# Eight of 206 weight blocks in a fused two-block kernel are loaded by two transfers, of 120 and of 8 partitions

## What is computed

```
def peer_ffn(hn, w_peer_q, sub_keys1, sub_keys2, expert_u, expert_v):
    # each token scores 128 x 128 product keys in 8 heads and keeps the best 16 of each head
    ...
    eidx = ...   # 128 experts of 16384 for each token
    def block(args):
        xt, e, g = args
        act = gelu(einsum('nkd,nd->nk', expert_u[e], xt))
        return einsum('nk,nkd->nd', g * act, expert_v[e])
```

## Time and profile before

| | |
|---|---|
| runs, us | 1340.96 median, 1339.92 to 1342.41 |
| the profiled execution's own time, us | 1340.73 |
| its span in the profile, us | 1339.0 |
| gathers (q0) | 268.45 MB, 48.4% of 16 DMA engines' span |
| weights and other loads (q1) | 112.05 MB, 25.4% |
| busy share of PE, DVE, ACT, POOL | 89%, 66%, 51%, 20% |

### The profile page before, as it was taken

How to read it: one execution, slowest core, us unless ns; L and a number is a source line. 1 busy time by engine, 2 the same in 40 slices (tenths; PEclk the granted TensorE clock), 3 DMA queues, 4 the chain that set the end, 5 groups by cost and what they waited for, 6 DMA issues and landing times.

```text
span 1339.0 us, 19013 instructions
## 1 busy us (share of the span) xinstructions
PE 1189.7 (89%) x6314; PEld 834.0 (62%) x6314; DVE 887.7 (66%) x1938; ACT 683.1 (51%) x1482; POOL 270.3 (20%) x305
## 2 busy tenths in 40 slices
PE   8999988887777878788879878999989999999998
PEld 6898864432222223233334323799989999999986
DVE  6764596667666667776667755576867657666664
ACT  6665555445444445554455543534446675444454
POOL 4000033333333333333333432000000030000000
PEclk9999989999999999899999999999999999999999
DMA  6322479999999999999999999536565346555563
GB/s 243 130 95 81 134 273 421 421 420 420 422 421 421 422 421 416 384 413 422 419 422 420 422 422 388 183 122 185 167 208 185 127 143 203 164 182 178 183 209 105
DMA packets 68652, 382.25 MB, mean 285 GB/s; under 512 B 7761, under 2 KB 7889, under 8 KB 35681
## 3 DMA queue, kind: packets, MB, share of 16 engines
q0 software_dynamic: 36864, 268.45, 48.4%
q1 hardware_dynamic: 31424, 112.05, 25.4%
q10 hardware_dynamic: 288, 0.82, 0.2%
HBM read 380.24 MB, written 1.05 MB: 285 GB/s over the span
## 4 chain that ended last, share of the span: by engine, by line
PE 51%; DMA 30%; DVE 8%; ACT 6%; issue 4%; POOL 0%; another core or an unknown queue 0%; SPq 0%; ACTq 0%; DVEq 0%
DMA work<-in_rows,work 30%; PE ps L572 27%; PE ps L915 9%; PE ps L1012 4%; DVE w_lo L367 2%; DVE work L2118 1%; ACT work L1427 1%; PE ps L606 1%; PE ps L826 1%; ACT work L1420 1%; PE ps L612 1%; PE ps L613 1%; ACT work L1423 1%; ACT w_hi L359 1%; DVE work L2311 1%
## 5 line engine op out<-in xcount | busy, mean ns | idle before, releaser
L915 PE MATMUL ps<-work 128*128 128x512 f32 x1024 | 501.8, 624 | 127.1 <-ACT work L1427 126.6
L2118 DVE CUSTOM_DVE_ANT_0 work<-work,ps 128x1024 f32<-128x1024 f32 x256 | 312.4, 1220 | 213.3 <-DMA work<-in_rows,work 210.2
L915 PEld LDWEIGHTS ps<-work 128*128 128x128 f32 x1024 | 182.6, 194 | 432.8 <-ACT work L1427 279.8
L510 POOL DMA_INDIRECT work<-in_rows,work x256 | 244.2, 954 | 566.4 <-PE ps L915 393.2
L367 DVE TENSOR_TENSOR w_lo<-ring,w_hi 128x1024 fp32r<-128x1024 f32 x206 | 252.4, 1231 | 118.6 <-ACT w_hi L359 117.0
L572 PE MATMUL ps<-x_lo,w_hi 128*128 128x256 f32 (+2 forms) x1224 | 294.0, 283 | 1.8 <-DVE x_lo L384 1.7
L359 ACT ACTIVATE w_hi<-ring 128x1024 fp32r<-128x1024 f32 x206 | 214.4, 1051 | 55.1 <-PE ps L1012 24.5
L1420 ACT ACTIVATE work<-work,peer_root 128x1 f32<-128x1 f32 x256 | 75.1, 294 | 317.9 <-DVE work L2118 316.3
L572 PEld LDWEIGHTS ps<-x_lo,w_hi 128*128 128x128 f32 x1224 | 229.0, 190 | 3.5 <-DVE x_lo L384 2.4
L572 PE MATMUL ps<-x_hi,w_hi 128*128 128x256 f32 (+2 forms) x760 | 187.3, 290 | 3.2 <-DVE w_lo L367 1.5
L572 PEld LDWEIGHTS ps<-x_hi,w_hi 128*128 128x128 f32 x760 | 140.7, 189 | 8.7 <-DVE w_lo L367 3.4
(11 more groups left out here) (364 smaller groups left out, 1238.2 us busy)
## 6 DMA issues: line engine op xcount, KB each, us to landing
ring<-in_stream SPq DMA_DIRECT2D x206, 512.0 KB, 3.7
work<-in_rows,work POOLq DMA_INDIRECT x256
res<-in_tokens SPq DMA_DIRECT2D x4, 272.0 KB, 3.2
gain_rows<-in_gain_rows SPq DMA_DIRECT2D x1, 1024.0 KB, 9.5
out_dram<-work SPq DMA_DIRECT2D x4, 256.0 KB, 2.3
keys_sb<-in_keys SPq DMA_DIRECT2D x1, 512.0 KB, 8.3
work<-in_gain ACTq DMA_DIRECT2D x1, 512.0 KB, 4.1
work<-in_kiwi ACTq DMA_DIRECT2D x1, 288.0 KB, 3.7
```

What stands on the lines that cost most here:

```text
L510: g.indirect_dma_start(out=gathered[:, n % ROWS, :], out_offset=None, in_=rows_dram, in_offset=bass.IndirectOffsetOnAxis(ap=expert[:, n:n ...
L915: last = mm(ps[:, Y_BANK[t] + j, :], diag[:, n % DIAGS, :], gathered[:, n % ROWS, D + 512 * j:D + 512 * j + 512], start=False, stop=k == S ...
L2118: v.tensor_tensor_reduce(R["product"][:, D * (n % 2):D * (n % 2) + D], gathered[:, n % ROWS, 0:D], ps[:, bank:bank + 2, :].rearrange("p b ...
```

## The change

Blocks 40 to 47 are taken out of SyncE's loop and each is loaded by two transfers, one of partitions 0 to 119 and one of partitions 120 to 127, the second on semaphores of its own (`rest_landed`). `split_hi` waits for both.

```
+MOST = P - 8
+SIDE = FIRST["w_in_2_values_0"]
...
+        rest_landed = [sem(f"rest_landed{i}") for i in range(RING)]
...
         def split_hi(act, b, turn=None):
             ...
             act.wait_ge(landed[k], t * 16 + 16 * (b // RING + 1))
+            if turn is None and SIDE <= b < SIDE + 2 * RING:
+                act.wait_ge(rest_landed[k], 16 * ((b - SIDE) // RING + 1))
...
-            for first, end in ((1, late), (late + 2, BLOCKS // RING)):
+            for first, end in ((1, SIDE // RING), (late + 2, BLOCKS // RING)):
                 ...
                 if first == 1:
+                    for b in range(SIDE, late * RING):
+                        sp.wait_ge(w_lo_ready, b + 1 - RING)
+                        sp.dma_start(ring[0:MOST, b % RING, :], stream[b][0:MOST, :]).then_inc(landed[b % RING], 16)
+                        sp.dma_start(ring[MOST:P, b % RING, :], stream[b][MOST:P, :]).then_inc(rest_landed[b % RING], 16)
                     for b in range(late * RING, (late + 2) * RING):
```

## The result

The changed kernel is slower: 1358.98 us, the median of 4 runs (1357.8 to 1361.91), against 1340.86 (1339.92 to 1342.41), the median of the three runs named above and a fourth; the ratio is 1.0136, with an interval of 1.0123 to 1.0149. The prediction was 1336.8 us, in a range of 1334.8 to 1342.8. The sign was wrong, and the time was missed by 22 us. All figures are of executions in the chip's usual state; a single one in a slower state (e12_from_last, 1381.08 us, with a granted TensorE clock of 0.846 in place of the 0.98 to 0.99 of its others) is left out.

The account below looks back on a forecast made before the run. The prediction took the gathers to be bound by the DMA engines, one late engine setting their end. Relieving it gave 3.4 + 2.0 - 1.3 = 4.1 us less, so 1336.8 us, in a range of 1334.8 to 1342.8.

Parts of the forecast that it names:

- What bounds the kernel: During the gathers: DMA engines bind, and one late engine sets the end, finishing about 3.4 us after the next.
- 10.5 worked out: Load of blocks 40 to 47: eight blocks at 1.31 us put 10.5 us on each engine, the late one too.
- No later step is shorter: Dot products after 243 us: an instruction packet lengthens a step by 0.94 us, which is never won back.
- I take the first: Split loads: the spared engine is the late one and sheds eight partitions a block, 10.5 us less work.
- 3.4 + 2.0 us of the sum: Gains in the gathers: 3.4 us until the next engine's end, 2.0 us from the stall at 562 us.
- the stall at 562 us: Gathers, when a gather waits for its buffer and other engines run dry: relief returns 0 to 2.6 us, taken as 2.0.
- The rival that the late engine is another: Split loads: the spared engine is not the late one; 1341.0 us, or 1342.3 with one partition more; chance 0.27.
- the term of a packet's price: Split loads: each partition costs its engine about 0.16 us; one more a block costs the next engine 1.3 us.
- Bytes: none added or removed: Loads of blocks 40 to 47: the split moves the same bytes as before.
- The slower rival: Split loads: small or both transfers fall on few engines, up to 10.4 us more, 1351.4 us; chance 0.06.
- The rule that I weighed as a rival: Split loads: both transfers spread over all 16 engines, so the late one sheds at most 0.6 us: 1340.3 us; chance 0.05.
- What was costed at nothing: SyncE's eight added issues (0.33 us each) and ScalarE's added semaphore (at most 0.3 us) hidden; work after the last row unchanged.

Follow-up runs that it names:

- e12_from_last: Changed kernel, but each of blocks 40 to 47 loaded whole after three small transfers reading rows 120 to 127 into partitions 0, 4 ... 28: 1343.96 us.
- e9_none: Changed kernel, but blocks 40 to 47 not loaded (a 16 x 16 float transfer in place of each): 1331.0 us.
- e14_own3: Changed kernel, but each of blocks 40 to 47 loaded whole after three small transfers of partitions 0, 4, 8: 1339.85 us, one run.
- e17_own5: Changed kernel, but each of blocks 40 to 47 loaded whole after three small transfers of partitions 0, 4 ... 16: 1346.68 us, one run.
- e5_evenodd: Changed kernel, but blocks 40 to 47 split into 64 even and 64 odd partitions: 1341.4 us.
- e18_every4: Changed kernel, but blocks 40 to 47 each loaded by four transfers of 32 partitions, every fourth one: 1341.1 us.
- e3_64_64: Changed kernel, but blocks 40 to 47 split into two halves of 64 neighbouring partitions: 1357.45 us.
- e19_near32: Changed kernel, but blocks 40 to 47 each loaded by four transfers of 32 neighbouring partitions: 1357.85 us.
- e15_own1: Changed kernel, but each of blocks 40 to 47 loaded whole after three small transfers of partition 0 alone: 1341.7 us, one run.
- e6: Changed kernel, but each of blocks 40 to 47 loaded whole after three small transfers of partitions 120 to 127: 1356.6 us.
- e11: Changed kernel, but each of blocks 40 to 47 loaded whole after three small transfers reading rows 0, 4 ... 28 into partitions 120 to 127: 1357.1 us.
- e7: Changed kernel, but each of blocks 40 to 47 loaded whole after three small transfers of partitions 0, 4 ... 28: 1345.47 us.
- e4: Changed kernel, but blocks 40 to 47 each loaded by two transfers of all 128 partitions, half the columns each: 1342.91 us.
- e8: Changed kernel, but each of blocks 40 to 47 loaded whole after three small transfers of partitions 0, 4 ... 24: 1344.89 us.
- e16: Changed kernel, but blocks 40 to 47 each loaded as 64 even, 60 odd and 4 odd partitions: 1349.47 us.

## Why the prediction was wrong

**What bounds the kernel** was read rightly in the main. The gathers are bound by the DMA engines, by one of them alone at the end, and what the blocks carry lies on that path: without them 10.1 us go, of 10.5 worked out (e9_none). Two readings on the way were off, without weight for the sum's sign: "No later step is shorter" is not so (12 of the steps after 243 us are under 2.44 us, the shortest 1.56; each follows one that was longer than 2.48 by about as much or more, so the 0.94 us do stay), and the late engine stands some 4 us behind the next and not 3.4, since by rows 4 the other engines' packets end at about 836.2 us and not at 837.0.

**The first step that failed** is "I take the first: one engine can be spared by this shape and one engine is late, and that they are the same is a choice, not a reading". They are not: the late engine is the fourth or fifth (e14_own3, e17_own5), and it is among the 15 engines of the large transfer. The 3.4 + 2.0 us of the sum, against the end of the next engine and in the stall at 562 us, never came up: the tail stayed, 4.4 us long. What a relieved engine would have given is open. The rival that the late engine is another had 0.27, far too little beside its own remark that 15 of 16 engines are of that kind. By that rival alone the time would have been 1342.3 us, inside the range, as the late engine also gets one of the small transfer's eight packets.

**The second, and the one that made the size,** is the term of a packet's price. "About 0.16 us for each partition" was taken from whole blocks and used for both transfers as if a packet cost the same wherever it goes. "Bytes: none added or removed" is true, and the throughput still fell from 422 to 298 GB/s. The large transfer costs 1.55 us a block beyond a whole block's load and the small one 0.59, 2.1 in all, where I had 0.16 for one more partition. That it is the layout over the partitions, and not the number of transfers, their size or the spared engine, is shown by e5_evenodd and e18_every4 against e3_64_64 and e19_near32. The prediction's list of what is added held instructions, semaphores and bytes, and no line for the order in which engines meet the partitions.

**The slower rival** reached up to 1351.4 us for another reason, that shares pile up on few engines. They don't: 15 and 8 completions stand in the records. Its number was short too, since it bounded an unknown by the packets' ordinary time. I called 10.4 us the upper bound "by the nearest rows", but those rows were all of one layout. A layout that no row shows was not bounded by them. (8 x 8 x 0.16 is 10.2, too, and not 10.4.)

**The rule that I weighed as a rival** (not to bother with two transfers) would have given 1340.3 us. Taken as a rule it pointed the right way, not to split; the price came from something else, as e5 and e18 are also split and free.

**What was costed at nothing** was nothing within some tenths of a us: SyncE's issues and its waits (e15_own1, +0.4), ScalarE's added semaphore (e5_evenodd with the same wait, +0.3), and the stretch behind the last row, 498.6 us in both kernels.

## What to carry to other kernels

Where a load runs beside another stream that fills the DMA engines, keep the layout over the partitions that the other stream has: all 128, or strided halves or quarters of them (60 of the 64 odd ones were not free). Neighbouring parts of a tile, even with the same bytes and the same number of transfers, cost 12 to 17 us in eight blocks here, and nothing where the DMA engines were otherwise free. Before sparing an engine, find out which one is late: small transfers on the first one, three, five and so on engines showed it here, in the steps at the blocks and in the tail.

## What the runs showed of the hardware

- Eight packets of 4 KB to eight neighbouring partitions held the gathers up by 0.60 to 0.61 us, to eight partitions four apart by 0.11 to 0.16 us, whatever was read (e6, e11, e7, e12).
- Loads in neighbouring parts lowered the throughput of all 16 engines from 422 GB/s to 298 (changed kernel) and 281 (e19), with the engines shown as busy as before; strided parts left it at 420 (e18).
- The split into 2 or 4 transfers as such cost the gathers nothing measurable (e4, e5, e18: -0.4 to +0.4 us).
- The DMA engine that was late was the fourth or fifth, by transfers of 1, 3, 5 and 7 partitions (e15, e14, e17, e8), if a smaller transfer's engines are also those of a larger one.
- A load left one completion for each engine that it used: 16 in the kernel before, 15 + 8 in the changed kernel, 16 + 15 + 4 in e16.
